# A layer's step loop on TensorE: each step's query projections put ahead of that step's weighted sums

## The reference

```python
def peer(h, wq, subkeys, u, v):
    q = (hf @ wq).reshape(n, PEER_HEADS, 2, D_KEY // 2)
    s = jnp.einsum('nhpd,pkd->nhpk', q, subkeys).astype(F32)
    top_s, top_i = lax.top_k(s, PEER_TOPK)
    ...                                   # best 16 of the 16 x 16 sums of two scores
    idx = i1 * N_KEYS + i2
    gate = jax.nn.softmax(best_s, axis=-1).astype(h.dtype)
    def expert_block(args):
        xb, ib, gb = args
        act = jax.nn.gelu(jnp.einsum('nd,nhkd->nhk', xb, u[ib]), approximate=False)
        return jnp.einsum('nhk,nhkd->nd', gb * act, v[ib])
```

## Time and profile before

| | us |
|---|---|
| median of three runs | 2641.35 |
| the profiled execution | 2640.45 |
| its span | 2638.1 |
| expert loop, layer 0 | about 425 to 1305 |
| expert loop, layer 1 | about 1735 to 2606 |
| TensorE busy | 2034.5 (77%) |
| VectorE busy | 1589.0 (60%) |
| POOL, ScalarE busy | 793.1 (30%), 697.5 (26%) |

### The profile page before, as it was taken

The page is one execution under the profiler, slowest core; times in us unless marked ns, Lnnn a source line. Parts: engine busy times, 40 slices in busy tenths (PEclk is TensorE's granted clock), DMA queues, the critical chain, the costliest instruction groups (busy, mean ns, idle before and its releaser), DMA issues.

```text
span 2638.1 us, 37877 instructions
## 1 busy us (share of the span) xinstructions
PE 2034.5 (77%) x11684; PEld 1183.5 (45%) x11684; DVE 1589.0 (60%) x4244; ACT 697.5 (26%) x1690; POOL 793.1 (30%) x831
## 2 busy tenths in 40 slices
PE   6999898888777666665779999988886776656565
PEld 4566687664343312211255667866652442211112
DVE  2544216666766788787634342365657678887875
ACT  2422213332222222222224222133313132222223
POOL 0022103233444344444201220023334433444441
PEclk9999999999898888788889999989998988888888
DMA  7134558999999999999752346499999999999996
GB/s 207 29 99 146 182 191 349 417 418 408 417 419 405 418 413 412 410 406 416 325 150 59 91 145 209 161 392 417 410 418 420 419 401 415 421 417 413 413 414 250
DMA packets 206463, 852.42 MB, mean 323 GB/s; under 512 B 19824, under 2 KB 91008, under 8 KB 124352
## 3 DMA queue, kind: packets, MB, share of 16 engines
q0 software_dynamic: 95280, 677.21, 62.4%
q1 hardware_dynamic: 110992, 172.89, 18.8%
HBM read 843.33 MB, written 6.71 MB: 322 GB/s over the span
## 4 chain that ended last, share of the span: by engine, by line
PE 24%; DMA 24%; issue 15%; DVE 12%; PEld 12%; PEldq 5%; DVEq 3%; ACT 2%; POOL 2%; ACTq 0%; POOLq 0%; SPq 0%
PE ps L727 9%; DMA MIX_RINGS<-in_peer_uv_dram,IDX 9%; DMA W<-in_peer_uv_dram,IDX 8%; DMA WQKV_E<-in_peer_uv_dram,IDX 6%; PEld ps L791 5%; PEldq L952 4%; PE ps L967 4%; PEld ps L950 3%; PE ps L739 3%; DVEq L1363 2%; DVE MIX_RINGS L1515 2%; PEld ps L856 2%; DVE W L1515 1%; PE ps L755 1%; PE ps L773 1%
## 5 line engine op out<-in xcount | busy, mean ns | idle before, releaser
L950 PE MATMUL ps<-MIX_RINGS,GC 64*64 64x512 f32 x3712 | 636.7, 690 | 207.7 <-ACT GC L1169 160.8
L675 POOL DMA_INDIRECT MIX_RINGS<-in_peer_uv_dram,IDX x400 | 441.0, 1103 | 791.1 <-PEq L952 444.9
L950 PE MATMUL ps<-W,GC 64*64 64x512 f32 x1840 | 384.7, 713 | 237.4 <-ACT GC L1169 216.3
L950 PEld LDWEIGHTS ps<-MIX_RINGS,GC 64*64 64x64 f32 x3712 | 181.3, 152 | 521.1 <-issue 521.1
L675 POOL DMA_INDIRECT W<-in_peer_uv_dram,IDX x182 | 201.0, 1105 | 435.6 <-PEq L952 359.7
L1169 ACT ACTIVATE GC<-twins,WV 128x64 f32<-128x64 f32 x640 | 170.4, 336 | 569.0 <-DVEq L1528 566.5
L1515 DVE CUSTOM_DVE_ANT_0 MIX_RINGS<-MIX_RINGS 128x1024 f32<-128x1024 f32 x224 | 268.4, 1223 | 77.6 <-DMA MIX_RINGS<-in_peer_uv_dram,IDX 69.6
L1515 DVE CUSTOM_DVE_ANT_0 MIX_RINGS<-MIX_RINGS,WQKV_E 128x1024 f32<-128x1024 f32 x176 | 213.0, 1224 | 158.6 <-DMA MIX_RINGS<-in_peer_uv_dram,IDX 151.7
L950 PEld LDWEIGHTS ps<-W,GC 64*64 64x64 f32 x1840 | 105.3, 154 | 441.3 <-issue 441.3
L727 PE MATMUL ps<-WQKV_E,HT 128*128 128x384 f32 x768 | 252.8, 486 | 0.7 <-issue 0.7
L1163 ACT ACTIVATE GV<-AV 128x4 f32<-128x4 f32 x160 | 32.9, 205 | 717.6 <-DVEq L1516 717.4
(11 more groups left out here) (257 smaller groups left out, 2741.5 us busy)
## 6 DMA issues: line engine op xcount, KB each, us to landing
W<-in_merge_w_dram SPq DMA_DIRECT2D x40, 1024.0 KB, 4.9
W<-in_merge_w_dram SPq DMA_DIRECT2D x60, 512.0 KB, 14.1
WQKV_E<-in_w_in_dram SPq DMA_DIRECT2D x48, 512.0 KB, 6.6
W<-in_query_w_dram SPq DMA_DIRECT2D x16, 1024.0 KB, 11.6
W<-in_w_in_dram SPq DMA_DIRECT2D x12, 1024.0 KB, 9.6
W<-in_query_w_dram SPq DMA_DIRECT2D x20, 512.0 KB, 9.4
W<-in_out_w_dram SPq DMA_DIRECT2D x8, 1024.0 KB, 14.4
MIX_RINGS<-in_peer_uv_dram,IDX POOLq DMA_INDIRECT x400, 13.4
```

Source lines behind the costliest of these rows:

```text
L675: pool.indirect_dma_start(UV[r], None, table, bass.IndirectOffsetOnAxis(IDX[:, n % 2, j:j + 1], 0))\
L950: pe.matmul(ps[o:o + CHUNK, n:n + 512], w[r, :], v[r, d * 512:(d + 1) * 512], start=False, stop=False, skip_group_check=True)
```

## The change

TensorE's list alone is written in another order. In every step, `first_queries` and `rest_queries` now stand between the step's chunk and its weighted sums (`experts`), where they stood behind the sums. The scores (`first_scores`, `rest_scores`), `rest_output` and the turning of the normed tiles stay behind the sums. No instruction is added or removed, and no wait is dropped. The variable `h` of the rest queries is now called `late`.

```diff
                     if s + AHEAD < CHUNKS:
                         chunk(l, s + AHEAD)
+
+                    h = AHEAD + s // 4
+                    if h < PH and s % 4 < 2:
+                        first_queries(l, h, s % 4)
+                    late, at = divmod(s - Q_STEP, 2)
+                    if 0 <= late < PH and at == 0:
+                        if late == 0:
+                            pe.wait_ge(*nt_ev.at(l, 2 * TILES * TURNS))
+                        rest_queries(l, late)
                     experts(l, s)
-                    h = AHEAD + s // 4
-                    if h < PH:
-                        if s % 4 < 2:
-                            first_queries(l, h, s % 4)
-                        if s % 4 == 2:
-                            first_scores(l, h)
+                    if h < PH and s % 4 == 2:
+                        first_scores(l, h)
                     if 0 <= s - OUT_STEP < GB:
                         rest_output(l, s - OUT_STEP)
                     if s == TURN_STEP:
                         norm_turn(l, 1, [1, 2])
-                    h, at = divmod(s - Q_STEP, 2)
-                    if 0 <= h < PH:
-                        if at == 0:
-                            if h == 0:
-                                pe.wait_ge(*nt_ev.at(l, 2 * TILES * TURNS))
-                            rest_queries(l, h)
-                        else:
-                            rest_scores(l, h)
+                    if 0 <= late < PH and at == 1:
+                        rest_scores(l, late)
```

## The result

With the change the kernel takes 2654.54 us (median, 2649.37 to 2659.62); the kernel before, run beside it, 2641.46 us (2639.3 to 2654.49). The ratio is 1.0043 with a 95% interval of 1.0033 to 1.0053: slower by 11.4 us (8.7 to 14.0). That is within the 1% that I called no change, and yet clear of the noise. The forecast was 2642 us with a range of 2630 to 2654. The side of 1% came out, the mechanism that bounds the loops did too, and the median lies half a microsecond above the range, because terms of the sum were wrong. The profiled execution of the changed kernel took 2654.82 us, its span is 2653.0 us.

A forecast was written before the change was run, and what follows sets the result against it. The prediction took bytes through the DMA engines to bound the loops. From the profiled 2640.45 us, -2.7 for earlier loads and +3.8 for the tile change gave 2641.6, forecast as 2642 us, range 2630 to 2654.

The forecast's parts named there:

- What bounds the loops: Both expert loops: bytes at 420 GB/s set the pace, not TensorE; 13.7 us counted per chunk step.
- The rivals that let TensorE set it or the rate rise: Both loops: TensorE sets the pace, 2604 us (0.03); or a steadier order draws 428 GB/s, 2580 us (0.03).
- The bulk of the moves at 0: Most query steps: delayed sums are hidden by the gathers POOL has queued ahead, so the moves cost 0.
- I leave it at 0: Step 13: the 4.10 us wait for the second half's weights, now ahead of the sums, costs 0.
- the rival of the dry gathers: Chunk steps: gathers run dry behind the query halves, 2.3 us each, 46 us in all, 2686 us; chance 0.05.
- SP's loads earlier, -2.7 us: Around steps 0 and 12: loads start 4.6 us earlier and regain half of 5.4 us of low-rate stretches.
- The tile change, +3.8 us: Step 32: queries wait for the cleared sums and delay POOL's gather 4.4 us; 1.9 us lost per layer.
- the bound of 4.4 without cover: Tile change: upper bound per layer, 4.4 us lost if SP's 1 MB load does not cover the later gather.
- The rival of the tile change in full: Step 32: SP's load comes too late to cover, 4.4 to 9.3 us twice, 2649 to 2659 us; chance 0.20.
- The signs: If right: loops at 413 GB/s or slightly over, odd sums directly behind even, tile-change stretch growing some 2 us per layer.

The follow-up runs named there:

- e9: The kernel before with seven of the eight terms of every moved query projection left out; 2641.92 us, ratio 1.0003.
- e11: The kernel before with half of each rest query's weights loaded, 512 KB in place of 1 MB; 2624.61 us, ratio 0.9927.
- e5: The changed kernel with step 16's query-half load issued ahead of the waiting output weights and the cleared-sums wait below the rest queries; 2640.74 us, ratio 1.0001.
- e3: The changed kernel with only the first tile's queries ahead of the sums, the rest queries back behind rest_output; 2646.63 us, ratio 1.0011.
- e1: The changed kernel with SP's load for step 16's query half issued a step earlier, ahead of the load that waits; 2648.05 us, ratio 1.0019.
- e4: The changed kernel with only the rest queries ahead of the sums, the first tile's queries back behind them; 2650.39 us, ratio 1.0025.
- e2: The changed kernel with the wait for the cleared sums of tile 1 below the rest queries; 2646.83 us, ratio 1.0013.
- e6: The kernel before with 8 do-nothing instructions at the start of TensorE's list; 2641.31 us, ratio 0.9999.
- e7: The kernel before with 100 do-nothing instructions at the start of TensorE's list; 2641.63 us, ratio 1.0002.
- e8: The kernel before, TensorE's list unchanged, with SP's query-half load of step 16 issued ahead of the output weights; 2641.06 us, ratio 0.9994.
- e12: The changed kernel with only step 16's query half put back behind its sums on TensorE, SP's list unchanged; 2653.33 us, ratio 1.0036.

## Why the prediction was half right

- **What bounds the loops: right, and shown.** Bytes set the pace (e9 and e11). The rivals that let TensorE set it or the rate rise are out: no slice of the strip lies over 421 GB/s, and the loops' rates fell. No order tried ran a loop at more than 414 GB/s (e5, 425 to 1300 us). The Trainium skill, DMA: Bandwidth & Descriptors, Specifications, gives 435 GB/s as the fabric ceiling; no loop of these kernels reached it.
- **The bulk of the moves at 0: right but for step 16.** e5 has every query ahead of its sums at 1.0001. From step 4 to step 12 the changed kernel's halves go from 484.56 to 593.93 us, 13.67 us per step, where the earlier trace rows give 13.75.
- **"I leave it at 0": the step that failed, though not where I put it.** I looked at the wait for a half's weights at step 13 alone; that one fell, from 4.10 us to 1.53. Three steps later the same kind of load stands behind one in SP's list that waits for TensorE's output projection. In the order of before that half found its weights there; asked for ahead of the sums, it did not. I had quoted that SP's list holds back what stands behind a waiting load, and had not walked it through for every half. Over both layers the runs price this at 2.9 us (e3) to 6.3 us (what e1 regains), where I had nothing. It is the rival of the dry gathers in one step of a layer in place of ten.
- **SP's loads earlier, -2.7 us: not regained.** The stretch at step 12 of layer 0 did improve (340 to 396 GB/s). But the gathers of step 14, issued just behind the earlier loads, took longer: the last of them was used 11.1 us after its issue (600.31 to 611.45), before 8.0 us (599.31 to 607.32). Its sums then waited 8.00 us, and so the load of step 16 came later. That the loads took the bytes from the gathers is my reading; no run tests it. The first queries as a whole came to +2.9 us (e3), and with both places mended e5 stands at +0.3 us (-2.1 to 2.6), not at -2.7.
- **The tile change, +3.8 us: the mechanism right, the size too small.** Measured are 5.0 us (2.9 to 7.4, what e1 leaves), 6.6 us (e4) and 7.9 us (what e2 regains), 2.5 to 4.0 per layer: between the 1.9 that I took and the bound of 4.4 without cover. What failed, as the trace has it, was the cover, SP's load behind these queries. SP had issued it by 842.44 us, behind their end at 841.88, when the dip (838 to 844 us at 119 GB/s) was mostly past; no run moved this load by itself. A load that the queries release can't fill a gap that the queries make. The rival of the tile change in full named that condition, "if no load lands in the gap", and had 0.20; its 2649 to 2659 us hold the measured time, in part by luck, since the tile change alone makes 2646 to 2649 us and the rest is step 16.
- **The range:** its high end was made of the tile change alone. With a few microseconds for one late load per layer it would have held.
- **The signs:** the loops' rates fell by 3 and 4 GB/s in place of staying. The low-rate stretch at the tile change grew by 2.0 and 1.8 us against 420 GB/s, as I had named it, and yet cost more time than that. The sums of odd rest-query steps didn't come directly behind those of the even ones: those of step 27, at 772.90 us, wait 3.46 us for their diagonals. New dips in every fourth step, the sign of the dry gathers, didn't come.

## What to carry to other kernels

When work is put ahead of the instruction that frees a buffer, moved time cost nothing in most steps of this kernel, where requests are queued ahead; look for the few steps in which a wait and the moved work come together in one gap, by walking each load that the moved work needs through its queue's whole list, not only the first one that looks late. Don't count as cover a transfer that the delaying work itself releases. And move a wait along with the work that needs it: at the tile change the wait belonged to the sums alone, and one line below the queries was worth 8 us.

## What the runs showed that I had not expected

TensorE can stall for up to 4.6 us (e1) in a loop with nothing in the profile to wait for. Neither another order of the work (e6, e7) nor another place in TensorE's own list (e8) is needed for it. What decides it, and whether it is the same in every execution, stays open, as each kernel has one trace. The view of TensorE's waits of the kernel before and of e6, whose order is the same (line, what it waited for: us in total, times, longest):

```profile
PE ps L950 <- issue: 74.3, 206, 0.5
```

```profile
PE ps L950 <- issue: 80.9, 203, 4.5
```

With eight instructions ahead of the program the longest is 4.5 us in place of 0.5. In e6, e7 and e8 that costs nothing, as TensorE has time to spare. That such a stall costs where it falls into a gap that is already long isn't excluded: e4, whose order at steps 15 to 17 is that of before, has stalls of 2.06 and 1.66 us there, POOL's wait of 13.29 us and 275 GB/s from 678 to 686 us; in e12 one of 2.01 us lies in the gap shown above. So some of the 6.6 us of e4 and of the 9.5 us of e12 may be theirs. What the engine waits for in them stays open.

No version that does all of the work beat the kernel before: the nearest, e8, has 0.9994 (0.9985 to 1.0003).
